# Block products for 8 of the 22 k tiles of a layer's down projection

## What is computed

```python
gu = jnp.einsum('btd,df->btf', h2, w_gate_up[l])
g, up = jnp.split(gu, 2, axis=-1)
x = x + jnp.einsum('btf,fd->btd', jax.nn.silu(g) * up, w_down[l])
```

## Time and profile before

| | |
|---|---|
| median of three runs | 2144.62 us |
| profiled execution, own time | 2143.96 us |
| its span, first to last instruction | 2142.2 us |
| TensorE busy | 2134.8 us, 12116 matmul records |
| VectorE busy | 1580.3 us |
| ScalarE busy | 1040.0 us |
| GpSimd busy | 130.3 us |
| granted TensorE clock, mean | 1.000 |

### The profile page before, as it was taken

The page is one execution under the profiler, slowest core; times in us unless marked ns, Lnnn a source line. Parts: engine busy times, 40 slices in busy tenths (PEclk is TensorE's granted clock), DMA queues, the critical chain, the costliest instruction groups (busy, mean ns, idle before and its releaser), DMA issues.

```text
span 2142.2 us, 31288 instructions
## 1 busy us (share of the span) xinstructions
PE 2134.8 (100%) x12116; PEld 1855.1 (87%) x12116; DVE 1580.3 (74%) x2452; ACT 1040.0 (49%) x1717; POOL 130.3 (6%) x177
## 2 busy tenths in 40 slices
PE   9999999999999999999999999999999999999998
PEld 7878889999888878889999888888888899888887
DVE  7999988888546999988788445664766579888723
ACT  5788565555324687565555323332544344222312
POOL 0010001110000110001110000000000000000000
PEclk9999999999999999999999999999999999999999
DMA  5221247775223211247775223223222231222222
GB/s 194 74 78 62 99 118 178 194 181 146 108 99 119 88 64 62 98 123 182 190 178 145 108 106 128 98 87 127 89 94 84 99 119 59 98 98 98 96 93 77
DMA packets 61177, 243.06 MB, mean 113 GB/s; under 512 B 7504, under 2 KB 8272, under 8 KB 45840
## 3 DMA queue, kind: packets, MB, share of 16 engines
q1 hardware_dynamic: 48112, 218.47, 29.1%
q0 software_dynamic: 12672, 23.07, 6.6%
q10 hardware_dynamic: 288, 0.14, 0.0%
HBM read 235.76 MB, written 2.10 MB: 111 GB/s over the span
## 4 chain that ended last, share of the span: by engine, by line
PE 99%; DMA 0%; DVE 0%; ACT 0%; SPq 0%; DVEq 0%; issue 0%
PE mm L2359 23%; PE mm L2361 23%; PE mm L2360 23%; PE sp L2359 7%; PE sp L2361 7%; PE sp L2360 7%; PE sp L2566 1%; PE ob L2594 1%; PE sp L2581 1%; PE ob L2574 1%; PE sp L2583 0%; PE ob L2360 0%; PE ob L2359 0%; PE ob L2361 0%; DMA w_raw<-in_w_dram 0%; PE misc L2360 0%
## 5 line engine op out<-in xcount | busy, mean ns | idle before, releaser
L2359 PE MATMUL mm<-in_hi,w_hi 128*128 128x512 f32 (+1 forms) x1520 | 536.5, 353 | 0.5 <-DVE in_lo L1432 0.5
L2361 PE MATMUL mm<-in_hi,w_lo 128*128 128x512 f32 (+1 forms) x1520 | 531.7, 350 | 0.0
L2360 PE MATMUL mm<-in_lo,w_hi 128*128 128x512 f32 (+1 forms) x1520 | 531.6, 350 | 0.0
L661 ACT ACTIVATE w_hi<-w_raw 128x2048 fp32r<-128x2048 f32 (+3 forms) x144 | 254.0, 1764 | 455.2 <-PE mm L2361 348.0
L1398 DVE TENSOR_TENSOR w_lo<-w_raw,w_hi 128x2048 fp32r<-128x2048 f32 (+2 forms) x143 | 312.1, 2184 | 193.5 <-ACT w_hi L661 192.2
L2359 PEld LDWEIGHTS mm<-in_hi,w_hi 128*128 128x128 f32 x1520 | 285.6, 188 | 41.2 <-issue 3.9
L2361 PEld LDWEIGHTS mm<-in_hi,w_lo 128*128 128x128 f32 x1520 | 285.6, 188 | 38.1
L2360 PEld LDWEIGHTS mm<-in_lo,w_hi 128*128 128x128 f32 x1520 | 285.7, 188 | 36.2
L1510 DVE SCALAR_TENSOR_TENSOR conv_y<-conv_in,parl,conv_y 128x512 f32<-128x512 f32 x240 | 169.7, 743 | 0.6
L2361 PE MATMUL sp<-in_hi,w_lo 128*128 128x512 f32 (+1 forms) x432 | 145.7, 337 | 0.0
L2359 PE MATMUL sp<-in_hi,w_hi 128*128 128x512 f32 (+1 forms) x432 | 145.7, 337 | 0.0
(11 more groups left out here) (503 smaller groups left out, 4467.5 us busy)
## 6 DMA issues: line engine op xcount, KB each, us to landing
w_raw<-in_w_dram SPq DMA_DIRECT2D x119, 1024.0 KB, 4.8
w_raw<-in_w_dram SPq DMA_DIRECT2D x85, 512.0 KB, 4.5
w_raw<-in_w_dram SPq DMA_DIRECT2D x32, 704.0 KB, 3.9
w_raw<-in_w_dram POOLq DMA_DIRECT2D x44, 256.0 KB, 4.0
w_third_sum<-in_w_dram SPq DMA_DIRECT2D x44, 256.0 KB, 4.8
w_third_sum<-in_w_dram POOLq DMA_DIRECT2D x44, 256.0 KB, 4.2
x<-in_x_dram SPq DMA_DIRECT2D x8, 256.0 KB, 6.3
out_dram<-z_rows SPq DMA_DIRECT2D x8, 256.0 KB, 2.0
```

Source lines behind the costliest of these rows:

```text
L661: e.activation(whi[:, slot, 0:cols], raw[:, slot, 0:cols], ACT.Copy).then_inc(s_whi, whi_out.up())
L2359: MM(out, ah, bh, start=first, stop=False, **kw)
L2360: MM(out, ah, bl, start=False, stop=False, **kw)
L2361: return MM(out, al, bh, start=False, stop=last, **kw)
```

## The change

For every pair p of output tiles the down projection now has two parts. The *plain part* does k tiles 12 to 21 and 8 to 11 as before, 2 x 14 tiles of 128 x 512. The *block part* does k tiles 0 to 7 by seven block products: operands are 4 k tiles by 256 tokens of the activations (or of one of four sums of such blocks, TD1 to TD4) and 4 k tiles by 128 channels of the weights (or of one of four sums, made in place in `w_raw`). Three partial results are copied out of PSUM by ScalarE and added by VectorE, which takes both output tiles of a pair together. Weights pass through a ring of eight spots of 4 tiles (512 columns); each part uses seven spots, 56 for the stage. The chunks of a plain part are 4 and 3 spots, that of a block part 4 quarters (1024 KB), from which the seven spots are made. Sums of activations and their splits are made once, at the beginning of the stage (i = 0 to 4 below). The loop of TensorE and SyncE is written out. Since the last pair uses other PSUM banks, `wide` waits for the last of them one step earlier.

The core of the diff, indentation cut down; sums and takes of the last pair, and the packing of the weights on the host, are left out:

```diff
-L_UG, L_KV, L_QG, L_GB, L_CO, L_OUT, L_GU, L_DOWN = 4, 2, 8, 4, 2, 4, 22, 16
+L_UG, L_KV, L_QG, L_GB, L_CO, L_OUT, L_GU, L_DOWN = 4, 2, 8, 4, 2, 4, 22, 12
...
-DOWN_ORDER = tuple(range(KEPT, FT)) + tuple(range(KEPT))
+BLOCK = 4
+PLAIN = tuple(range(KEPT, FT)) + tuple(range(2 * BLOCK, KEPT))
+DOWN_STEPS = tuple((blocks, p) for p in range(4) for blocks in (False, True))
+RING, N_SPOTS = 8, 7
+DOWN_CHUNKS = tuple(n for blocks, _ in DOWN_STEPS for n in ((7,) if blocks else (4, 3)))
+DOWN_ENDS = tuple(itertools.accumulate(DOWN_CHUNKS))
+D_SPOTS = DOWN_ENDS[-1]
+BLOCK_AT = (0, 3, 3, 3, 1, 2, 0)
+UP_FREES = (0, 1, 3, 4, 5, 6, 2, 7)
...
+TD4, TD1, TD2, TD3 = range(4)
+sum_11, sum_w = spf[1][:, 0:TH], spf[1][:, T:T + TH]
+def down_bank(p):
+  return (four[0], four[1]) if p % 2 == 0 else (four[3], four[2])
+def down_sum(t, o):
+  return t[:, 2 * o:2 * o + 2, :].rearrange("p a (b c) -> p (a b) c", b=2)
+def down_spot(n):
+  blocks, p = DOWN_STEPS[n // N_SPOTS]
+  return blocks, p, n % N_SPOTS
+def down_raw(n):
+  blocks, _, j = down_spot(n)
+  c = next(i for i, end in enumerate(DOWN_ENDS) if n < end)
+  q = BLOCK_AT[j] if blocks else n - (DOWN_ENDS[c] - DOWN_CHUNKS[c])
+  return c, raw[:, c % 2, quarters[q]]
+def spot_freed(n):
+  return UP_FREES[n] if n < RING else n
...
-load_free(n + (L_CHUNKS - L_DOWN), 0, operands.now(-1), HALF)
+load_free(n + (L_CHUNKS - L_DOWN), 0, operands.now(-1))
 operands.skip(5)
-load_free(n + (L_CHUNKS - L_DOWN + 1), 1, operands.now(-1), HALF)
+load_free(n + (L_CHUNKS - L_DOWN + 1), 1, operands.now(-1), DOWN_CHUNKS[1] * OP)
 operands.skip(2)
-stage(n + (L_CHUNKS - L_DOWN + 2), L_DOWN // 2 - 1, (HALF, HALF))
-load(n + L_CHUNKS, 0)
-load(n + (L_CHUNKS + 1), 1)
+for c in range(2, L_DOWN + 2):
+  cols = DOWN_CHUNKS[c] * OP if c < L_DOWN and DOWN_CHUNKS[c] == 3 else CH
+  load_free(n + (L_CHUNKS - L_DOWN + c), c % 2, operands.now(-DOWN_ENDS[c - 2]), cols)
+operands.skip(D_SPOTS)
...
# ScalarE
+up_done = done.now()
+def spot_done(n):
+  e.wait_ge(s_sm, up_done + 7 + n + 1)
+def spot_high(n):
+  blocks, _, j = down_spot(n)
+  c, src = down_raw(n)
+  if n == DOWN_ENDS[c] - DOWN_CHUNKS[c]:
+    landed(c % 2)
+  if blocks and j in (2, 3, 5, 6):
+    e.wait_ge(s_ds, sums.now(-{2: 1, 3: 3, 5: 2, 6: 4}[j]))
+    if j == 6:
+      sums.skip(4)
+  e.wait_ge(s_sm, up_done + spot_freed(n))
+  high_of(n % RING, src)
+def block_copy(i, dst):
+  spot_done(i)
+  e.activation(dst, sum_11, ACT.Copy).then_inc(s_sc, copies.up())
+def down_sum_high(o):
+  e.wait_ge(s_val, val.next())
+  hi(down_sum(xh, o), down_sum(xf, o))
+def next_high(m):
+  hi(xh[:, m, :], x[:, m, :], parl[:, m + A_GN:m + A_GN + 1])
+def x_squares(p, final=False):
+  e.wait_ge(s_val, val.next(2))
+  if final:
+    next_high(2 * p)
+    next_high(2 * p + 1)
+  for d, m in enumerate((2 * p + 1, 2 * p)):
+    squared(m, d)
...
+for n in range(3):
+  spot_high(n)
+e.wait_ge(s_sm, up_done + 4)
+kept_high(2 * BLOCK)
+kept_high(2 * BLOCK + 1)
 silu()
+kept_high(2 * BLOCK + 2)
 act_high(FT - 1)
+spot_high(3)
+kept_high(2 * BLOCK + 3)
+for n in range(4, RING):
+  spot_high(n)
+done.skip(7 + D_SPOTS)
+for i in range(D_SPOTS):
+  blocks, p, j = down_spot(i)
+  final = p == KT // 2 - 1
+  if i == 0:
+    hi(acth[:, 0:BLOCK, first_half], actf[:, 0:BLOCK, first_half])
+  if i == 1:
+    hi(acth[:, BLOCK:2 * BLOCK, :], actf[:, BLOCK:2 * BLOCK, :])
+  if i == 2:
+    down_sum_high(TD1)
+    down_sum_high(TD2)
+  if i == 3:
+    down_sum_high(TD3)
+    down_sum_high(TD4)
+  if blocks and j == 0:
+    if p:
+      e.wait_ge(s_mmf, taken.now(-2 * p))
+    block_copy(i, tD[:, first_half])
+  if blocks and j == 3:
+    block_copy(i, tD[:, second_half])
+  if blocks and j == 5:
+    block_copy(i, tC[:, first_half])
+  if i + RING < D_SPOTS:
+    spot_high(i + RING)
+  if j == 1 and i > N_SPOTS and DOWN_STEPS[i // N_SPOTS - 1][0]:
+    x_squares(DOWN_STEPS[i // N_SPOTS - 1][1])
...
+landed(1)
+spot_done(D_SPOTS - 1)
+prep_part(1, slice(0, CH))
+x_squares(KT // 2 - 1, True)
...
# VectorE
+def spot_low(n):
+  blocks, _, j = down_spot(n)
+  c, src = down_raw(n)
+  low_of(n % RING, src)
+  a11, a12, a21, a22 = (raw[:, c % 2, q] for q in quarters)
+  if blocks and j == 1:
+    e.wait_ge(s_so, operands.now())
+    TT(a22, a21, a22, ALU.add).then_inc(s_ds, wsums.up())
+    e.wait_ge(s_ds, wsums.now())
+    TT(a21, a11, a21, ALU.subtract).then_inc(s_ds, wsums.up())
+  if blocks and j == 2:
+    e.wait_ge(s_so, operands.now())
+    TT(a22, a22, a11, ALU.subtract).then_inc(s_ds, wsums.up())
+    e.wait_ge(s_ds, wsums.now())
+    TT(a11, a12, a22, ALU.subtract).then_inc(s_ds, wsums.up())
+spot_low(0)
+spot_low(1)
+kept_low(2 * BLOCK)
 gate_takes(FT - 1, 6)
+kept_low(2 * BLOCK + 1)
 last_silu = fn.next()
+spot_low(2)
+kept_low(2 * BLOCK + 2)
 act_of(FT - 1, FT - 1, 7, val, last_silu)
 act_low(FT - 1)
+kept_low(2 * BLOCK + 3)
+for n in range(3, RING):
+  spot_low(n)
+b11, b12 = actf[:, 0:BLOCK, first_half], actf[:, 0:BLOCK, second_half]
+b21, b22 = actf[:, BLOCK:2 * BLOCK, first_half], actf[:, BLOCK:2 * BLOCK, second_half]
+def down_sum_low(o):
+  lo(down_sum(xl, o), down_sum(xf, o), down_sum(xh, o), kept)
+def second_row_takes(p):
+  e.wait_ge(s_sc, copies.now(-3))
+  TT(tC[:, second_half], sum_w, tC[:, first_half], ALU.add).then_inc(s_do, own.up())
+  e.wait_ge(s_val, val.now())
+  e.wait_ge(s_do, own.now())
+  TT(tB[:, 0:T], down_bank(p)[1], tC[:], ALU.add).then_inc(s_mmf, taken.up())
+def first_row_takes(p, i):
+  e.wait_ge(s_sm, up_done + 7 + i + 1)
+  TT(tA[:, 0:T], down_bank(p)[0], tD[:], ALU.add).then_inc(s_mmf, taken.up())
+  for t in (tB, tA):
+    TT(t[:, 0:T], t[:, 0:T], rstd[:], ALU.mult).then_inc(s_do, own.up())
+  for m, t, back in ((2 * p + 1, tB, 1), (2 * p, tA, 0)):
+    e.wait_ge(s_do, own.now(back))
+    TT(x[:, m, :], x[:, m, :], t[:, 0:T], ALU.subtract).then_inc(s_val, val.up())
+  copies.skip(3)
+for i in range(D_SPOTS):
+  blocks, p, j = down_spot(i)
+  final = p == KT // 2 - 1
+  if i == 0:
+    TT(down_sum(xf, TD1), b12, b11, ALU.subtract).then_inc(s_val, val.up())
+    e.wait_ge(s_val, val.now())
+    TT(down_sum(xf, TD2), b22, down_sum(xf, TD1), ALU.subtract).then_inc(s_val, val.up())
+  if i == 1:
+    TT(down_sum(xf, TD3), b22, b12, ALU.subtract).then_inc(s_val, val.up())
+    e.wait_ge(s_val, val.now(1))
+    TT(down_sum(xf, TD4), b21, down_sum(xf, TD2), ALU.subtract).then_inc(s_val, val.up())
+  if i == 2:
+    e.wait_ge(s_val, val.now())
+    lo(actl[:, 0:BLOCK, first_half], b11, acth[:, 0:BLOCK, first_half], kept)
+    lo(actl[:, BLOCK:2 * BLOCK, :], actf[:, BLOCK:2 * BLOCK, :], acth[:, BLOCK:2 * BLOCK, :], kept)
+  if i == 3:
+    down_sum_low(TD1)
+    down_sum_low(TD2)
+  if i == 4:
+    down_sum_low(TD3)
+    down_sum_low(TD4)
+  if blocks and j == 3:
+    e.wait_ge(s_sc, copies.now(-2))
+    TT(tD[:, second_half], sum_w, tD[:, second_half], ALU.add).then_inc(s_do, own.up())
+  if blocks and j == 5:
+    second_row_takes(p)
+  if blocks and j == 6:
+    first_row_takes(p, i)
+  if i + RING < D_SPOTS:
+    spot_low(i + RING)
...
+in_lo(KT - 2, col(parl, KT - 2 + A_GN))
+in_lo(KT - 1, col(parl, KT - 1 + A_GN))
 last_square()
 prep_and_sum()
...
# TensorE
+def plain_part(p, n):
+  bank = down_bank(p)
+  if p > 1:
+    e.wait_ge(s_mmf, taken.now(-2 * p))
+  for t in range(BLOCK * N_SPOTS):
+    d, j = t // len(PLAIN), t % len(PLAIN)
+    k, a = PLAIN[j], slice(t % BLOCK * P, t % BLOCK * P + P)
+    if t % BLOCK == 0:
+      operand(n + 1)
+    if p == 0 and j == 0:
+      e.wait_ge(s_sv, products.now(0 if d else 3))
+    if p == 0 and d == 0:
+      told = kept if k < KEPT else sub
+      e.wait_ge(told.sem, told.next())
+    ins = mm3(bank[d], spot(whi, n % RING)[:, a], spot(wlo, n % RING)[:, a],
+         acth[:, k, :], actl[:, k, :], j == 0, j == len(PLAIN) - 1)
+    if t % BLOCK == BLOCK - 1:
+      ins.then_inc(s_sm, done.up())
+      n += 1
+def block_times(out, n, hi_, lo_, start):
+  operand(n + 1)
+  for k in range(BLOCK):
+    a = slice(k * P, k * P + P)
+    ins = mm3(out, spot(whi, n % RING)[:, a], spot(wlo, n % RING)[:, a], hi_[:, k, :], lo_[:, k, :],
+         start and k == 0, k == BLOCK - 1, skip_group_check=True)
+  ins.then_inc(s_sm, done.up())
+def acts(k, half):
+  return acth[:, k:k + BLOCK, half], actl[:, k:k + BLOCK, half]
+def sums_of(o):
+  return down_sum(xh, o), down_sum(xl, o)
+def block_part(p, n):
+  first, second = down_bank(p)
+  if p == 0:
+    e.wait_ge(s_cv, kept.now(-1))
+  e.wait_ge(s_sc, copies.now())
+  block_times(sum_11, n, *acts(0, first_half), True)
+  if p == 0:
+    e.wait_ge(s_cv, kept.next(6))
+  block_times(second[:, first_half], n + 1, *sums_of(TD4), False)
+  if p:
+    e.wait_ge(s_mmf, taken.now(-(2 * p + 1)))
+  block_times(sum_w, n + 2, *sums_of(TD1), True)
+  e.wait_ge(s_sc, copies.now(-1))
+  block_times(sum_11, n + 3, *sums_of(TD2), False)
+  block_times(first[:, first_half], n + 4, *acts(BLOCK, first_half), False)
+  e.wait_ge(s_sc, copies.now(-2))
+  block_times(sum_11, n + 5, *sums_of(TD3), False)
```

(71 more changed lines are left out.)

25 lines of the change are left out of this document (5 added, 20 removed).

## The result

The kernel after takes 2165.45 us, the median of 6 runs (2164.76 to 2165.96). The kernel before, beside it, takes 2144.37 us (6 runs, 2143.77 to 2144.68). The ratio is 1.0098, with a 95% interval of 1.0088 to 1.0108: slower. The forecast was 2163.3 us, in a range of 2156 to 2169. The median is 20.8 us above the 2144.62 us of the kernel before on record with the forecast; 18.7 was forecast. The profiled execution took 2164.76 us, and its own span is 2162.9 us against 2142.2.

A forecast was written before the change was run, and what follows sets the result against it. TensorE was taken as the bound, busy 2134.8 of 2142.2 us. Per layer -3.8 + 10.2 + 0.95 + 2.0 = +9.35 us, +18.7 for both, gave 2163.3 us, range 2156 to 2169.

The forecast's parts named there:

- The matmuls saved: Down projection, TensorE: 48 matmuls of 512 columns become 84 of 256 per pair, saving 3.8 us a layer.
- VectorE's order: Start of down projection: VectorE's queued work and waits delay the first block part's operands, costing TensorE 10.2 us a layer.
- The wait at the load: Start of down projection: VectorE stands 3.8 us at spot 7's low, whose 1024 KB load lands late, with activation sums queued behind.
- The gaps: First block part: TensorE stands 3.7 us before the first product and 6.5 us after it, 10.2 us a layer.
- The clock: Behind the long gap TensorE may fall to half pace, costing 2.6 us a layer or nothing; 2.0 taken.
- The end of the stage: Next stage's start waits for the last pair's second take, behind four queued `in_lo` on VectorE: 0.95 us a layer.
- The ring in the steady state: Later parts of the down projection: spots are refilled in time, cost nothing; without cover, about 1 us per block part.
- the rival of a starved ring: TensorE also waits about 1 us in the other six block parts and before plain parts: 2175 us; within a shared 10%.
- the steady clock: Rival: the stall in the down projection comes but the clock doesn't fall, 2159.3 us; chance 20%.
- Splits in time: Rival: first block part's operands are ready in time, only saving and stage end count, 2138.9 us; chance 6%.

The follow-up runs named there:

- experiment 2: Kernel after with two plain parts ahead of the first block part (plain 0, plain 1, block 0, block 1, then by turns): 2139.87 us, ratio 0.9978.
- experiment 3: Kernel after with 28 and 52 unused matmuls of 256 columns ahead of the first block part's two waits: 2160.11 us, ratio 1.0072.
- Experiment 1: Kernel after with sums and highs of activations moved ahead of spot 7's low and high, which wait for a load: 2157.13 us, ratio 1.006.
- Experiment 5: On experiment 2, two of the four lows ahead of the last pair's takes moved behind them: 2138.8 us, ratio 0.9975.
- experiment 4: Kernel after with 8 MB of unread zeros behind the weights in HBM, making the array as large as before: 2164.86 us, ratio 1.0093.

## Why the prediction was right, step by step

- **The matmuls saved.** -3.8 us a layer was forecast. In experiment 2 TensorE has no other wait in the stage than that at its end, and its stage is 2.78 us shorter than before; with the 1.0 us of the end taken off, -3.78. The pace from start to start, and not the mean duration of records, was the right measure.
- **VectorE's order.** The count of 26.9 us of work and 5.95 us of waits put the tenth `kept` 33.27 us behind 526.08. Measured it is 560.07 - 526.57 = 33.50 us. The wait at the load is 3.98 us instead of 3.8. The gaps, over the pace, are 3.9 and 6.4 us (forecast 3.7 and 6.5), together 10.3 against 10.2; experiment 3 has 10.4. Experiment 1 shows the term for the load. Experiment 2 shows that the time of the first use decides: VectorE's work up to the tenth `kept` is there still 27.8 us behind the start of the stage, and TensorE doesn't wait. The split of the remaining 6.3 us into work and shorter waits stays a count.
- **The clock.** 2.0 us a layer was forecast from the launch; 1.73 and 2.01 were measured. The 2.0 was a choice between nothing and 2.6, so that it came out so close is partly luck. That the launch shows the same thing isn't shown: its window reads a granted clock of 1.00 and this one 0.51. Nor did the fall follow the long gap, as the prediction had it: it came before that gap began (last section), and the clock was still low behind it. The Trainium skill (TensorE: Matmul & The Clock Gate, section Why this matters for your kernels) warned of gaps of a few microseconds, and the runs agree: the granted clock came down to 0.50 with gaps of 3.68, 3.76 and 6.26 us.
- **The end of the stage.** 0.95 us forecast, 1.0 measured (1.12 from start to start, less 0.12). Experiment 5 halves it by moving half of the queue.
- **The ring in the steady state.** Cost at nothing, and so it is: the takes of the pairs stand at 570.16, 599.15 and 628.13, 29.0 us apart, and TensorE has no wait in the other six block parts. So the rival of a starved ring (2175) falls too. One price of the prediction's steady state was wrong: two of the four sums of weights were taken at 0.60 us each and last 1.7, because they coincide with work of GpSimd (last section). The slack held it.
- **What was not priced.** The two stages are 19.03 us longer, against 18.7. The other 1.67 of the 20.7 us had no term in the sum: 0.49 ahead of layer 1's stage, where executions of the same kernel differ by as much (528.72 and 529.38 us in the two traces of the kernel before), 0.09 behind the two layers, and 1.09 in layer 2 ahead of its down projection (experiment 4). The prediction looked at nothing outside the stage that it changed.

The other two rivals: the steady clock (2159.3) falls by experiment 3, which shows what that would be, 2160.11. Splits in time (2138.9) is what another order of the steps makes: 2139.87.

## What to carry to other kernels

Before matmuls are traded for work of another engine, lay that engine's written order against the first use of each of its results; a share of busy time says nothing of it. Where the first use comes too early, change the order of TensorE's own steps first: one line turned 1.0098 into 0.9978. And look for a step that waits for a load ahead of steps that need nothing of it.

## What the runs showed of the hardware

- The clock did not fall where the slow matmuls are. The granted clock in windows of the kernel after (us, busy us and instructions of PE, PEld, DVE, ACT, POOL, granted clock, DMA share, GB/s), in layer 1 the short gap, the first product and the long gap, then the same three in layer 2:
```profile
548.40:552.10 3.70, 0.02 (x1) 0.00 (x0) 3.63 (x6) 1.91 (x4) 0.00 (x0) 1.00 0.00 0
552.20:553.90 1.70, 1.70 (x12) 1.46 (x12) 1.70 (x1) 1.70 (x4) 0.00 (x0) 0.93 0.00 0
554.00:560.10 6.10, 0.00 (x0) 0.00 (x0) 6.10 (x8) 1.70 (x4) 0.00 (x0) 0.50 0.00 0
```
```profile
1199.60:1203.40 3.80, 0.13 (x1) 0.00 (x0) 3.73 (x6) 2.01 (x4) 0.00 (x0) 0.84 0.01 2
1203.40:1206.20 2.80, 2.79 (x12) 2.63 (x12) 2.80 (x3) 2.74 (x5) 0.00 (x0) 0.50 0.00 0
1206.20:1211.30 5.10, 0.14 (x1) 0.00 (x0) 5.10 (x6) 0.90 (x2) 0.00 (x0) 0.50 0.00 0
```
  In layer 1 the clock stayed up through the short gap and came down at the end of the first product, between 553.50 and 553.75 us, when TensorE had been at work again for 1.5 us. In layer 2 it came down inside the short gap, between 1202.0 and 1202.5 us, and stayed down through the first product and the long gap. So two gaps of the same length differ in when the fall comes, and it can come after work has begun again. In experiment 1, with the long gap alone, it came inside that gap in both layers.
- The first matmuls behind the two gaps of layer 2:
```profile
1203.41 0.58 PE L2527 MATMUL sp<-act_hi,w_hi 128*128 128x256 f32 x1 [3.68 <-DVE act_lo L1526]
...
1211.36 0.58 PE L2527 MATMUL mm<-in_hi,w_hi 128*128 128x256 f32 x1 [5.02 <-DVE in_lo L1526]
```
  The first product's twelve follow at 0.213 us, and in layer 1 at 0.118. That cost nothing, since the second wait took it up: it is 5.02 us here and 6.20 in layer 1.
- At the lower clock 256 columns take 0.213 us, 1.80 times 0.1183 and not twice. Behind the second gap it lasted for 17 matmuls in layer 1 and 21 in layer 2 (3.8 and 4.6 us).
- In all the clock was low for some 10 us in layer 1 and 13.5 in layer 2, the long gaps included. In a row whose slices are 54 us the second is one digit lower and the first isn't seen. Both are found in windows of a few us, or by the length of the records (0.41 against 0.28).
- A step of VectorE that reads two tensors lasts longer while GpSimd adds. The same sum of weights (L2065) lasts 0.69 us at 549.58, where GpSimd is idle, and in the next block part:
```profile
577.93 1.76 DVE L2065 TENSOR_TENSOR w_raw<-w_raw 128x512 f32<-128x512 f32 x1
```
```profile
577.85 2.99 POOL L625 TENSOR_TENSOR ssum<-ssum,sq 128x512 f32<-128x512 f32 x2 [65.21 <-ACT sq L719]
```
  It is so again at 606.93 and 635.91 (1.67 us), each time beside GpSimd's two adds.
